# Blocked products by token tile beside three normalizations of a fused transformer block

## What is computed

```python
x = x + gt_a * (mix @ w_o)                                  # job "wo", 4 column chunks
h = rmsnorm(x, norm_ffn) * (1 + sc_f) + sh_f                # normalization t = 2
gate, up = split(h @ w_gate_up, 2)                          # jobs "gate", "up"
x = x + gt_f * ((silu(gate) * up) @ w_down)                 # jobs "down"
x = rmsnorm(x, final_norm)                                  # normalization t = 3, with
h = rmsnorm(x, a_norm_2)                                    # the one behind it
u, v, gate2 = split(h @ a_w_in_2, 3)                        # jobs "v2", "u2", "g2"
y = gelu(u) * (w_s applied to rmsnorm(gelu(v)) + b_s)
x = x + (y * silu(gate2)) @ a_w_out_2                       # jobs "wout"
return rmsnorm(x, final_norm_2)                             # normalization t = 5
```

## Time and profile before

| | before |
|---|---|
| median of 3 runs | 2352.28 us (2351.45 to 2353.06) |
| profiled execution | 2351.64 us |
| its span, first to last instruction | 2350.3 us |
| PE busy | 2270.8 us, 97%, 10867 matmuls |
| DVE busy | 1510.1 us, 64% |
| ACT busy | 1010.5 us, 43% |
| POOL busy | 19.3 us, 1% |
| mean granted TensorE clock | 0.987 |
| read from HBM | 500.41 MB, 214 GB/s |

### The profile page before, as it was taken

How to read it: one execution, slowest core, us unless ns; L and a number is a source line. 1 busy time by engine, 2 the same in 40 slices (tenths; PEclk the granted TensorE clock), 3 DMA queues, 4 the chain that set the end, 5 groups by cost and what they waited for, 6 DMA issues and landing times.

```text
span 2350.3 us, 27129 instructions
## 1 busy us (share of the span) xinstructions
PE 2270.8 (97%) x10867; PEld 1873.3 (80%) x10867; DVE 1510.1 (64%) x1897; ACT 1010.5 (43%) x1258; POOL 19.3 (1%) x25
## 2 busy tenths in 40 slices
PE   5999999999999989999999999998999999999997
PEld 3688898788888868888888888886888888888886
DVE  6888888878768777755554455466555555555555
ACT  4345444333444454443344434445444444444343
POOL 0000000000000000000000000000000000000000
PEclk9999999999999989999999999998999999999999
DMA  9976747665887768765555555554655555555553
GB/s 362 355 248 205 233 162 253 217 200 185 282 289 273 265 221 287 263 225 186 196 180 192 186 195 180 196 179 160 207 191 190 184 190 195 183 187 194 189 195 109
DMA packets 276156, 504.64 MB, mean 215 GB/s; under 512 B 24000, under 2 KB 38080, under 8 KB 275264
## 3 DMA queue, kind: packets, MB, share of 16 engines
q1 hardware_dynamic: 276032, 502.93, 63.0%
HBM read 500.41 MB, written 2.49 MB: 214 GB/s over the span
## 4 chain that ended last, share of the span: by engine, by line
PE 85%; DVE 8%; issue 2%; ACT 2%; DMA 2%; SPq 1%; POOL 0%; DVEq 0%; ACTq 0%
PE bank L1074 25%; PE bank L1075 25%; PE bank L1076 25%; DVE WL L1774 2%; PE bank L1268 2%; DVE GA L1757 1%; PE bank L996 1%; PE bank L1086 1%; PE bank L1088 1%; PE bank L1087 1%; PE bank L1023 1%; DVE A L1986 1%; ACT WH L1355 1%; PE bank L1019 1%; PE bank L1240 1%
## 5 line engine op out<-in xcount | busy, mean ns | idle before, releaser
L1774 DVE TENSOR_TENSOR WL<-RAW,WH 128x1024 fp32r<-128x1024 f32 (+1 forms) x728 | 882.0, 1218 | 637.0 <-ACT WH L1355 633.4
L1355 ACT CAST WH<-RAW 128x1024 fp32r<-128x1024 f32 (+1 forms) x728 | 757.7, 1047 | 898.0 <-PE bank L1076 723.5
L1074 PE MATMUL bank<-WH,HTh 128*128 128x512 f32 x1984 | 790.9, 399 | 8.7 <-issue 5.0
L1076 PE MATMUL bank<-WH,HTl 128*128 128x512 f32 x1984 | 775.6, 391 | 0.0
L1075 PE MATMUL bank<-WL,HTh 128*128 128x512 f32 x1984 | 775.4, 391 | 0.0
L1074 PEld LDWEIGHTS bank<-WH,HTh 128*128 128x128 f32 x1984 | 374.4, 189 | 92.4 <-issue 11.2
L1075 PEld LDWEIGHTS bank<-WL,HTh 128*128 128x128 f32 x1984 | 374.4, 189 | 79.7 <-issue 4.8
L1076 PEld LDWEIGHTS bank<-WH,HTl 128*128 128x128 f32 x1984 | 374.0, 189 | 78.8
L1757 DVE SCALAR_TENSOR_TENSOR GA<-RAW,ST,GA 128x512 f32<-128x512 f32 x264 | 181.1, 745 | 16.0 <-DMA RAW<-in_w_ada_dram 10.7
L1074 PE MATMUL bank<-WH,R2h 128*128 128x512 f32 x408 | 164.4, 403 | 3.8 <-DVE R2l L2096 3.0
L1076 PE MATMUL bank<-WH,R2l 128*128 128x512 f32 x408 | 159.9, 392 | 0.0
(11 more groups left out here) (254 smaller groups left out, 1678.8 us busy)
## 6 DMA issues: line engine op xcount, KB each, us to landing
RAW<-in_a_w_in_dram SPq DMA_DIRECT2D x96, 1024.0 KB, 5.1
RAW<-in_w_gate_up_dram SPq DMA_DIRECT2D x88, 1024.0 KB, 5.0
RAW<-in_w_ada_dram SPq DMA_DIRECT2D x80, 1024.0 KB, 5.4
RAW<-in_w_in_dram SPq DMA_DIRECT2D x63, 1024.0 KB, 4.9
RAW<-in_w_down_dram SPq DMA_DIRECT2D x44, 1024.0 KB, 5.0
RAW<-in_a_w_out_dram SPq DMA_DIRECT2D x32, 1024.0 KB, 5.0
A<-in_w_ada_dram SPq DMA_DIRECT2D x16, 1024.0 KB, 10.6
RAW<-in_w_o_dram SPq DMA_DIRECT2D x16, 1024.0 KB, 5.1
```

Source lines behind the costliest of these rows:

```text
L1074: e.matmul(o, ah[:, s], hi[:, k, :], start=first, stop=False)
L1076: i = e.matmul(o, al[:, s], hi[:, k, :], start=False, stop=last)
L1355: e.copy(hi, rv).then_inc(S["hi"], 1)
L1774: e.tensor_tensor(lo, rv, hi.bitcast(F32), ALU.subtract).then_inc(S["lo"], 1)
```

## The change

The jobs beside the three normalizations no longer take both token tiles half by half. `wo` 3, `gate` 0, `down` (2, 3), `v2` 0 and `wout` (3, 3) go through `run_blocks`: a block of halves for token tile 0, then the same halves for tile 1. `blocks` gives the sizes: 8 halves (all) for `wo` 3 and `gate` 0, 6 (all) for `down` (2, 3), 6, 1 and 1 for `v2` 0, and 4 (all) for `wout` (3, 3). The halves of a block are kept until tile 1 has used them, so `WH` and `WL` get extra places: four in `A` for `wo` 3 and `gate` 0, two in the unused `R2h` and `R2l` for `down` (2, 3) and `v2` 0. A half goes to the free place that has been free longest, and `fill` stages as long as a place is free. The residual, squares, sum, power, transposes, broadcast and normalized input of the last chunk are done for each token tile by itself (`done_tile`, `turn_last`): tile 0's while PE goes through tile 1 of the same job, tile 1's while PE goes through tile 0 of the next job. PE signals the end of tile 0 by a semaphore `tile` of its own. The transposes of chunk 2 and of the tiles, the broadcast and the groups now stand between passes in PE's queue. The last normalization's product with `final_norm_2` for the last chunk comes behind its sum, DVE takes 1280 and ACT 768 columns of each tile at the end, and the four output transfers are two for each tile. The constant -0.5 for the power comes with the other constants and not from a memset. `load_fn` stands one job earlier. A product of a half over one token tile is called a pass below.

```diff
+EXTRA_A, EXTRA_R = (4, 5, 6, 7), (8, 9)
...
+    last_wo, last_down, last_wout = d1[3], ffn[-1], g2[-1]
+    last_wo.blocks, last_wo.extra, last_wo.early = (8,), EXTRA_A, 1
+    ffn[0].blocks, ffn[0].extra = (8,), EXTRA_A
+    last_down.blocks, last_down.extra, last_down.early = (6,), EXTRA_R, 2
+    g2[0].blocks, g2[0].extra = (6, 1, 1), EXTRA_R
+    last_wout.blocks, last_wout.early = (4,), 3
...
+        self.places = [(self.WH[:, n, :], self.WL[:, n, :]) for n in range(NHL)]
+        self.places += [(self.over(f"WHx{n}", 24 + 8 * n, 1024, FR), self.over(f"WLx{n}", 28 + 8 * n, 1024, FR)) for n in range(4)]
+        self.places += [tuple(f[:, 1024 * n:1024 * n + 1024] for f in flat) for n in range(2)]
...
+        place = self.free_place(j)
+        self.place.append(place)
+        self.after.append(self.user[place] + 1)
+        self.user[place] = hid
...
+    def free_place(self, j):
+        n = min(tuple(range(NHL)) + j.extra, key=lambda n: self.user[n])
+        return n if self.user[n] < self.used else None
+
+    def fill(self, most):
+        for _ in range(most):
+            if self.staged[0] == len(self.units):
+                return
+            u = self.units[self.staged[0]]
+            if self.free_place(u[1] if u[0] == "w" else self.halves[-1][0]) is None:
+                return
+            self.stage_next()
...
     def consume(self, j, where):
-        while len(self.halves) < self.used + NHL and self.staged[0] < len(self.units):
-            self.stage_next()
+        self.fill(8)
...
+    def run_blocks(self, j):
+
+        self.current = pr = 1 - self.current
+        self.finish(self.pending[pr])
+        self.left = self.total = sum(j.blocks)
+        first, steps = self.used, 2 * self.total
+        for n, size in enumerate(j.blocks):
+            for tt in range(2):
+                for hid in range(first, first + size):
+                    self.fill(2)
+                    while len(self.halves) <= hid:
+                        self.stage_next()
+                    hj, t0, nk = self.halves[hid][:3]
+                    assert hj is j
+                    for k in range(nk):
+                        self.settle(self.need(j, t0 + k, tt))
+                    self.put("half", hid, pr, tt)
+                    self.used += tt
+                    steps -= 1
+                    self.left = (steps + 1) // 2
+                    if hid + 1 == first + size and n + 1 == len(j.blocks):
+                        j.end = self.used
+                        if j.early:
+                            self.done_tile(j, pr, tt)
+                        elif tt:
+                            self.retire(j, pr)
+                    self.slot()
+            first += size
+
+    def done_tile(self, j, pr, tt):
+        t, r, c = {"wo": (2, 0, j.c), "down": (3, 3, 3), "wout": (5, 7, 3)}[j.name]
+        if tt == 0:
+            for g in self.turn_bg:
+                self.finish(g)
+            if t < 5:
+                self.settle(("gta" if t == 2 else "gtf", 3))
+            if t == 2:
+                for q in range(4):
+                    self.settle(("mod", 9 + 2 * q))
+        self.put("res", r, c, pr, tt)
+        self.bg.append(self.turn_last(t, tt))
...
+    def turn_last(self, n, bb):
+
+        self.put("turn_sq", n, 3, (bb,))
+        yield
+        if n == 5:
+            self.put("turn_rs", n, bb, self.ms())
+            self.put("end", bb, self.ms_n)
+            return
+        if n == 3:
+            self.ms()
+        self.put("turn_rs", n, bb, self.ms())
+        m = self.ms_n
+        yield
+        self.put("turn_t", n, 3, bb)
+        yield
+        self.put("turn_b", n, bb, m - (n == 3))
+        for g in range(5):
+            self.put("turn_g", n, bb, g)
             if g:
-                self.have |= {(prefix, 2 * g - 2), (prefix, 2 * g - 1)}
-            if g == 8:
-                if n == 2:
-                    self.bg.append(self.spread("gtf", 20))
-                else:
-                    self.put("x3")
-            if g > 3:
-                yield
+                self.have |= {("h2" if n == 2 else "h3", 4 * g - 4 + k, bb) for k in range(4)}
+            yield
+        if bb and n == 2:
+            self.bg.append(self.spread("gtf", 20))
+        elif bb:
+            self.put("x3", m)
...
-        for j in J["d"]:
+        for j in J["d"][:-1]:
             self.run(j)
-        self.settle(("gta", 3))
         self.put("load_fn")
-        for g in self.turn_bg:
-            self.finish(g)
-        self.put("turn_rs", 2, self.ms())
-        self.marks["rs2"] = self.ms_n
-        for q in range(4):
-            self.settle(("mod", 9 + 2 * q))
-        self.bg.append(self.turn_tiles(2, "h2"))
+        self.run_blocks(J["d"][-1])
+        self.turn_bg = []
+        self.run_blocks(J["ffn"][0])
+        for j in J["ffn"][1:-1]:
+            self.run(j)
+        self.run_blocks(J["ffn"][-1])
+        self.turn_bg = []
+        self.run_blocks(J["gmlp"][0])
+        for j in J["gmlp"][1:-1]:
+            self.run(j)
+        self.run_blocks(J["gmlp"][-1])
         self.slot()
-        self.turn_bg = []
-        for j in J["ffn"]:
-            self.run(j)
-        for g in self.turn_bg:
-            self.finish(g)
-        self.put("turn_rs", 3, self.ms(), self.ms())
-        self.marks["rs3"] = self.ms_n
-        self.bg.append(self.turn_tiles(3, "h3"))
-        self.slot()
-        self.turn_bg = []
-        for j in J["gmlp"]:
-            self.run(j)
-        for g in self.turn_bg:
-            self.finish(g)
-        self.put("turn_rs", 5, self.ms())
-        self.put("end", self.ms_n)
+        assert not self.bg, self.bg
...
-                    for tt in range(2):
+                    for tt in tiles:
...
-            i.then_inc(S["half"], 1)
+            if tiles[-1] == 1:
+                i.then_inc(S["half"], 1)
+            elif t0 + nk == j.nkt and j.early:
+                i.then_inc(S["tile"], 1)
...
-            t, = args
-            W.wait_ge("turn_d", 2 * t - 2)
-            take(7)
-            e.matmul(bank[7][:, 0:T], ones, L.DR, start=True, stop=True).then_inc(S["turn_b"], 1)
-            held[7] = [(f"t{t}_m", 8)]
+            t, bb, _ = args
+            W.wait_ge("turn_d", 2 * t - 3 + bb)
+            take(4 + bb)
+            e.matmul(bank[4 + bb][:, 0:P], ones, L.DR[:, bb * P:(bb + 1) * P], start=True, stop=True
+                     ).then_inc(S["turn_b"], 1)
+            held[4 + bb] = [(f"t{t}_m", 4 * bb + 4)]
...
-            W.wait_ge("half", hid - NHL + 1)
+            W.wait_ge("half", sch.after[hid])
+            if sch.place[hid] >= NHL:
+                W.wait_ge(*extra_free(sch, sch.place[hid]))
...
+def tile_free(sch, t, bb):
+
+    return ("half", job_end(sch, *(("wo", 3) if t == 2 else ("down", (2, 3))))) if bb else ("tile", t - 1)
+
+
+def extra_free(sch, place):
+
+    return ("mx", 16) if place in EXTRA_A else ("half", job_end(sch, "og", 3))
...
-            W.wait_ge("half", job_end(sch, name, jc))
+            if args[3:] == (0,):
+                W.wait_ge("tile", {0: 1, 3: 2, 7: 3}[n])
+            else:
+                W.wait_ge("half", job_end(sch, name, jc))
...
+            ops, i, ts = (4 if t == 2 else 1), 4 * bb + g, slice(bb * P, (bb + 1) * P)
+            W.wait_ge(*tile_free(sch, t, bb))
+            if g < 4:
+                rb = bank[4 + bb][:, 0:P].unsqueeze(1).to_broadcast([P, 4, P])
+                W.wait_ge("turn_b", 2 * t - 3 + bb)
+                W.wait_ge("turn_x", turn_x_value(t, g, bb if g == 3 else 1))
+                W.wait_ge(f"t{t}_hi", ops * (i - 1))
+                W.wait_ge(f"t{t}_lo", ops * (i - 1))
+                e.tensor_tensor(L.TM[i % 2].rearrange("p (k t) -> p k t", t=P), L.XT[:, 4 * g:4 * g + 4, ts], rb, ALU.mult
                                 ).then_inc(S[f"t{t}_m"], 1)
...
+            for name, hs in (("out_d", slice(0, 1280)), ("out_a", slice(1280, 2048))):
+                W.wait_ge(name, bb + 1)
+                e.dma_start(out[bb * P:(bb + 1) * P, hs], X[:, bb, hs]).then_inc(S["out"], 16)```

The first place is DVE's queue from the residual of `wo` 1 to that of `wo` 2; L1774 (L1890 in the change) is the low part of a weight half, L1757 (L1871) a `GA` step, L2119 and L2121 (L2238, L2240) the residual. Before:

```order
L2121 TENSOR_TENSOR A<-A 128x512
L1774 TENSOR_TENSOR WL<-RAW,WH 128x1024 x3
L1757 SCALAR_TENSOR_TENSOR GA<-RAW,ST,GA 128x512 x4
L1774 TENSOR_TENSOR WL<-RAW,WH 128x1024 x4
L1757 SCALAR_TENSOR_TENSOR GA<-RAW,ST,GA 128x512 x4
L1774 TENSOR_TENSOR WL<-RAW,WH 128x1024
L2119 TENSOR_TENSOR A<-bank,A 128x512
```

242 lines of the change are left out of this document (121 added, 121 removed).

## The result

| | before | after |
|---|---|---|
| median | 2352.28 us (2350.70 to 2353.06, 5 runs) | 2361.26 us (2360.47 to 2363.49, 5 runs) |
| ratio, 95% interval | | 1.0041 (1.003 to 1.0052) |
| span of the profiled execution | 2350.3 us | 2359.9 us |
| mean granted clock | 0.987 | 0.988 |

A forecast was written before the change was run, and what follows sets the result against it. PE, busy 97% of the span, was taken as the bound, with gains only where it idles or runs at the lower clock. Terms 15.3 + 4.5 - 4.0 = +15.8 us gave 2368 us, range 2361 to 2373.

The forecast's parts named there:

- A: First normalization, PE's transposes of columns 1024 to 1535: PE waits 7.2 us for DVE's residual, held up by a load.
- What costs nothing: Items counted as free: the `neg_half` constant (one POOL memset less), four more POOL power operations, an unchanged number of transfers.
- PE's busy time higher only by that: Sign expected in the changed profile: PE's busy time grows only through stretches at 0.50 clock around 825, 845 and 860.
- B: First normalization, broadcast of tile 0's factors: PE waits 3.1 us, behind two DVE subtractions for `gate` 0.
- C: First normalization, transposes of tile 1: DVE's queue takes 23.7 us against PE's 10.0, so 13.7 us are lost.
- D: First normalization, broadcast of tile 1's factors: 0.9 us of wait plus some slower clock, 2.2 us lost.
- The first normalization in sum: Stage from `wo` 3 to `up` 0: 27.8 us lost against 12.5 before, so +15.3 us.
- The second: Normalization beside `down` (2, 3) and `v2` 0: 16.6 us lost against 12.1 before, +4.5, between +1 and +6.
- The end: From the last product to the span's end: tile 1 ready sooner and less to write, -4.0 us, between -3 and -5.
- That the new waits stay away: Rival: DVE's queue from first broadcast to tile 1's residual is short enough to cover the normalizations, 2324 us; 4 in 100.
- That the load is no bar: Rival: at the transposes of columns 1024 to 1535 the load comes in time, 7 to 9 us less, about 2360; 14 in 100.
- That the clock falls more often: Rival: several waits per normalization each bring a slow-clock stretch, up to 4 us more, 2372; 20 in 100.

The follow-up runs named there:

- x2: The change with 32 unused bytes ahead of arena `A`, undoing its shift against 64 bytes: 2369.29 us, ratio 1.0072.
- x1: The kernel before with 32 unused bytes ahead of arena `A`, nothing else moved: 2344.53 us, ratio 0.997.
- x9: The change with at most four weight halves staged ahead during `wo` 0 to `wo` 2, as before: 2358.31 us, ratio 1.0035.
- x5: The change with no weight half staged ahead during the first five passes over tile 1 of `wo` 3 and `down` (2, 3): 2357.00 us, ratio 1.0022.
- x3: The kernel before with only the change's last-normalization part, plus the constant that moves `A`: 2342.72 us, ratio 0.9962.
- x8: The kernel before with the tile-by-tile end, the moved `A`, and the last weight half staged ahead of `wout` (3, 2)'s residual: 2341.68 us, ratio 0.9955.
- x10: The kernel before with 96 unused bytes ahead of arena `A`, which then starts 64 past a multiple of 128: 2350.93 us, ratio 0.9999.

## Why the prediction came out as it did

**The measured 2361.26 lies in the range, at its lower edge, and 6.7 below the forecast.** The direction and the waits came out as the walk has them; that the number is still inside the range is luck, since its lower end was meant for a load in time at A, which did not happen. The step that failed stands under "What costs nothing": the `neg_half` constant. The text counted the memset that goes and not the eight words that come, which move the arena by 32 bytes. That is a gain of 6.2 us in the stage of the eleven `down` jobs, shown by undoing it in the change (x2: 2369.29, +17.4) and by making it alone (x1: -7.3). No view of before shows it as a wait; it could be read only as two distances between products, 0.2333 in `down` and 0.2267 elsewhere. The prediction's own 0.2275 was taken in `wo` 3 alone (its rows, 839.75 to 840.43 for three, give 0.2267; over 32 passes that is 0.2 us). And PE's busy time falling from 2270.8 to 2264.0 in a slower kernel contradicts the line "PE's busy time higher only by that": 6.2 of it are gone from the `down` jobs and 4.7 ahead of `wo` 3, where this execution had the full clock for longer; the other stages add 4.2.

**A, the transposes of columns 1024 to 1535:** 7.2 forecast, 6.8 measured, by the path that was walked (the load behind two subtractions, cast, subtraction, residual): issue at 815.66, cast at 820.87, subtraction at 822.05, residual from 823.19. The walk had PE go on at 828.9, which is 826.3 with the earlier start of 2.6 us; it was 825.98. (The rows named for the 5.1 us of a load show 4.95; the page has 5.1 as the median.) x9 shows that the order accounts for half of the wait only.

**B, the first broadcast:** 3.1 forecast, 2.8 measured. x5 took the two subtractions away and the wait went, as "without them PE would have it at E+4.2" says.

**C, the transposes of tile 1:** "as a wait of about 12": 12.1. PE's broadcast to the transposes: 23.7 forecast, 23.8 measured (844.22 to 868.00). The chosen 0.27 for ACT's 128-column operations was too small for those with a bias. Four of L1684 take 1.28 us, so they are 0.30 apart:

```profile
845.52 1.28 ACT L1684 ACTIVATE HTh<-A,MOD 128x128 fp32r<-128x128 f32 x4 [2.88 <-issue]
```

The Trainium skill (ScalarE: Activation LUTs, What ACT_TABLE_LOAD costs) gave, as an estimate from its figures, 0.29 us. The trace agrees with it. The rounds of cast and subtraction took 4.17 to 4.21 us instead of 4.04, which is 0.4 in sum; the whole still came out within 0.1, since the four `GA` steps and what stands ahead of them took 0.2 less than in the walk, and the 0.2 that the walk adds for hand-overs did not show. The 0.26 for DVE's low parts was right (four take 1.13).

**D, the broadcast of tile 1:** 0.9 of wait forecast, 0.5 measured.

**The first normalization in sum:** +15.3 forecast, +15.6 measured. **The second:** +4.5 forecast, +5.4 measured, with waits of 6.4 (5 forecast), 3.1 (3.4) and 1.3 (1.7). **The end:** -4.0 forecast, -3.3 measured, and PE waits 0.3 us (0.9 in x3) for a late last half that the walk had left out; x8 takes this wait away.

**The rivals.** That the new waits stay away (0.04) is refuted by the list of waits. That the load is no bar (0.14) is refuted by the wait of 6.8, though the time came out near its 2360, for another reason: right number, wrong mechanism. That the clock falls more often (0.20) has rows for it, such as 0.59 and 0.50 from 856.5 to 872, and in the first stage the mean granted clock was 0.84 against 0.89 before. But the sums of the two stages leave no more than 0.3 and 0.9 us for it beyond what the walk had counted; how much of that is the clock, no run separates.

## What to carry to other kernels

Walk each in-order queue between two points where another engine needs it, in its listed order and with durations from rows; the share of busy time (64% for DVE here) said nothing of the 12 us that PE waited for it, and moving the same work (x5) gained 4.3 us. Before a walk is summed, list what the change does to addresses too: a constant that grows moves all that is placed behind it. When most of a forecast's stages agree and the sum does not, compare job by job; the difference then has a place, and often another cause than the one in dispute.

## What was not expected of the hardware

The distance between 512-column products of a 128x128 stationary operand was 0.2267 us when both operands began, as far as their arena goes, at a multiple of 128 bytes in their partition, and 0.2333 us (2.9% more) when one of them lay in an arena that began 32, 64 or 96 bytes past one. It holds for the stationary operand at all three (`aTh`: 96 in the kernel before, 64 in x10, 32 in x2) and for the moving one at 32 (`WHx`, x2), at full granted clock, and no wait is listed for it. Why it is so stays open. Other offsets were not tried, nor one of the products with both operands off such a multiple.
